# The first four output tiles of each layer computed as two pairs in Strassen's block form

## The chip, the cores and the metric

The kernel runs on one core of one Trainium2 chip. The metric is the device time of one execution in microseconds, before the change the median of three runs. A trace of one profiled execution exists beside these runs, and all durations of single instructions below come from it.

## What is computed

The reference is one inference step of a two-layer decoder trunk on 592 tokens (16 meta tokens, 512 prompt tokens, 8 x 8 sample tokens), width 1024, all in float32. Of each layer only the last two lines matter for the change:

```python
merged = jax.nn.sigmoid(g_a) * (o_a @ w_a) + jax.nn.sigmoid(g_b) * (o_b @ w_b)
return x + merged @ w_o, S_new, conv_new, h_last
```

Here `merged` is 592 x 1024, `w_o` is 1024 x 1024 and `x` the layer's input. The next layer (and the end) begins with an RMSNorm of the result, which needs the sum of squares over all 1024 features. In the second layer the 16 meta tokens are dropped, so its late stages work on 576 tokens.

## The kernel before

**Layout and precision.** Features lie on the 128 partitions: a tensor of width 1024 is 8 tiles (k = 0 to 7) of 128 features by 592 tokens. The tokens are cut in two halves of 296 (288 in the second layer), one PSUM bank per tile and half. Each float32 operand is split into a high part (rounded to the matmul's format by ScalarE) and a low part (the rest, by VectorE), and every product is three matmuls into one bank: high x high, low x high, high x low. Names: `w_raw` is the weight as loaded, `w_hi` and `w_lo` its parts; `xn_hi` and `xn_lo` hold the right operand.

**Weights.** They come in units of 1024 columns (eight 128 x 128 blocks, 512 KB) through a ring of four slots. SyncE (SP) loads unit u into its slot when unit u - 4 is done, ScalarE makes `w_hi` (L524, `split_hi`), VectorE makes `w_lo` (L531, `split_lo`), three units ahead of TensorE.

**The stages at the end of a layer**, in TensorE's order:

1. Gate stage, four pairs of tiles (`product`, L2275 to L2286). It is already in the block form: the 2 x 2 blocks of a pair's weights (A11, A12, A21, A22) and of the right operand are combined so that 7 block products of 12 matmuls take the place of 8. Sums of weight blocks are made in place: S1 and S3 by an accumulating DMA that GpSimd issues onto a block in `w_raw` (L773), S2 and S4 by VectorE (`part_add`, L1778). The combined right operands are `diff`, `mix2`, `edge` and `last_right`. The weight blocks are half units (128 x 512, 256 KB) in a ring of eight: block n is loaded when block n - 8 is done (L608), its high part is L1103 (`part_high`), its low part L1769 (`part_low`). A bank in which a partial sum stands is read before the next product is added to it.
2. Stage B: 8 tiles (m), 72 matmuls each (12 blocks x 2 halves x 3). VectorE multiplies each half by the gate out of PSUM (L1864), adds it to `acc` (L1868, this is `merged`), ScalarE makes `xn_hi` of it (L1179) and VectorE `xn_lo` (L1854, `low_merged`), one tile late.
3. Stage O, the output projection `merged @ w_o`: 8 tiles, 8 blocks x 2 halves x 3 = 48 matmuls each. Tiles 0 and 1 run interleaved (`project_first`). VectorE adds each half from PSUM, times 0.5, to x (`new_x`, L1882), which GpSimd has loaded again into `acc` (L778). Then, for the next layer, ScalarE makes `xg_hi` (L820) and the squares (L810), VectorE the low part `xg_lo` (L1240) and the running sum of squares (L1235). In the second layer the last four tiles run half by half.
4. The next layer begins with `project_first` on `xg`, and in its midst `square_sums` (L2005), which needs the sum of squares of tile 7.

Every engine works through its own list in the order written. Nothing reorders it, so an instruction that waits holds up everything behind it on its engine.

## Time and profile before

| | |
|---|---|
| median of 3 runs | 1902.77 us (1902.31 to 1903.42) |
| the profiled execution | 1901.83 us, span 1900.0 us |
| TensorE busy | 1880.8 us, 99% |
| VectorE busy | 1262.8 us, 66% |
| ScalarE busy | 807.3 us, 42% |
| GpSimd busy | 284.6 us, 15% |
| DMA, mean over the span | 136 GB/s |

The table is read from the top: TensorE is busy nearly all the time, and the others have room on average. But a matmul's row shows its whole latency of about 0.30 us, while the next one starts about 0.136 us after it, so that rows overlap. What a matmul costs is the distance between starts. An average over the span also hides that VectorE is close to full in some stages.

### The profile page before, as it was taken

Reading aid. Unit: us, or ns where it says so; the run is one execution under the profiler, and the core shown is the slowest. Engines: PE = TensorE matmul, PEld = TensorE weight load, DVE = VectorE, ACT = ScalarE, POOL = GpSimd, SP = SyncE. Lnnn points to the kernel's source line nnn. Section 1 sums busy time; section 2 is a strip of 40 time slices with the busy share of each in tenths; the row PEclk is TensorE's granted clock in tenths of the full one; section 3 lists DMA queues with packets and bytes.
Section 4 is the critical chain, followed back from the end, with each engine's and each line's share of the span. In section 5 each row is a group of like instructions: output and inputs, shape, how many; then the busy total and the mean of one; then the engine's idle time right before and its main releaser. Section 6 shows DMA issues by size and latency. Waiting matters only on the chain.

```text
span 1900.0 us, 32236 instructions
## 1 busy us (share of the span) xinstructions
PE 1880.8 (99%) x12984; PEld 1762.9 (93%) x12984; DVE 1262.8 (66%) x2144; ACT 807.3 (42%) x1293; POOL 284.6 (15%) x399
## 2 busy tenths in 40 slices
PE   8999999999999999999999999999999999999998
PEld 7899898898899999999998988988989999999997
DVE  8775665665766877864487656657557678878445
ACT  5432332423427776542344324234124377766223
POOL 2221120120231200100022201202102422001000
PEclk9999999999999999999999999999999999999999
DMA  6435544453443333543354445534544533327332
GB/s 219 129 125 166 160 149 128 164 178 110 149 150 93 107 104 97 154 124 120 99 174 158 147 124 172 178 110 149 169 126 137 165 102 111 95 83 193 103 123 78
DMA packets 114786, 257.48 MB, mean 136 GB/s; under 512 B 11822, under 2 KB 52254, under 8 KB 114510
## 3 DMA queue, kind: packets, MB, share of 16 engines
q1 hardware_dynamic: 84350, 156.00, 26.4%
q0 software_dynamic: 30144, 99.41, 16.5%
q8 instruction: 103, 1.69, 0.4%
q14 instruction: 45, 0.37, 0.1%
q10 hardware_dynamic: 144, 0.00, 0.0%
HBM read 196.55 MB, written 49.12 MB: 129 GB/s over the span
## 4 chain that ended last, share of the span: by engine, by line
PE 87%; DVE 5%; ACT 3%; DMA 2%; DVEq 1%; issue 1%; ACTq 1%; SPq 0%
PE bank L1944 20%; PE bank L1946 20%; PE bank L1945 20%; PE bank L2014 4%; PE bank L2015 4%; PE bank L2016 4%; PE last L2032 2%; DMA w_raw<-in_w_units 1%; PE last L2014 1%; PE last L2015 1%; PE last L2016 1%; PE bank L2282 1%; PE bank L2285 1%; PE bank L2284 1%; PE sums L2147 1%
## 5 line engine op out<-in xcount | busy, mean ns | idle before, releaser
L1944 PE MATMUL bank<-xn_hi,w_hi 128*128 128x296 f32 (+1 forms) x2176 | 650.8, 299 | 0.4 <-DVE w_lo L531 0.3
L1946 PE MATMUL bank<-xn_lo,w_hi 128*128 128x296 f32 (+1 forms) x2176 | 646.4, 297 | 0.0
L1945 PE MATMUL bank<-xn_hi,w_lo 128*128 128x296 f32 (+1 forms) x2176 | 645.7, 297 | 0.0
L1944 PEld LDWEIGHTS bank<-xn_hi,w_hi 128*128 128x128 f32 x2176 | 409.2, 188 | 7.0 <-issue 4.3
L1945 PEld LDWEIGHTS bank<-xn_hi,w_lo 128*128 128x128 f32 x2176 | 409.6, 188 | 1.0
L1946 PEld LDWEIGHTS bank<-xn_lo,w_hi 128*128 128x128 f32 x2176 | 408.8, 188 | 0.0
L524 ACT ACTIVATE w_hi<-w_raw 128x1024 fp32r<-128x1024 f32 x229 | 241.0, 1056 | 347.0 <-DMA w_raw<-in_w_units 344.5
L531 DVE TENSOR_TENSOR w_lo<-w_raw,w_hi 128x1024 fp32r<-128x1024 f32 x229 | 280.7, 1229 | 88.9 <-ACT w_hi L524 82.1
L1944 PE MATMUL bank<-oa_hi,w_hi 128*128 128x296 f32 (+1 forms) x512 | 153.7, 300 | 0.0
L1945 PE MATMUL bank<-oa_hi,w_lo 128*128 128x296 f32 (+1 forms) x512 | 151.9, 297 | 0.0
L1946 PE MATMUL bank<-oa_lo,w_hi 128*128 128x296 f32 (+1 forms) x512 | 151.7, 296 | 0.0
L1944 PE MATMUL bank<-ob_hi,w_hi 128*128 128x296 f32 (+1 forms) x384 | 114.0, 297 | 0.0
L1945 PE MATMUL bank<-ob_hi,w_lo 128*128 128x296 f32 (+1 forms) x384 | 113.9, 297 | 0.0
L1946 PE MATMUL bank<-ob_lo,w_hi 128*128 128x296 f32 (+1 forms) x384 | 113.8, 296 | 0.0
L2014 PE MATMUL bank<-w_hi,xn_hi 128*128 128x512 f32 x256 | 100.9, 394 | 0.7 <-DVE rot_k L1368 0.7
L2016 PE MATMUL bank<-w_lo,xn_hi 128*128 128x512 f32 x256 | 100.8, 394 | 0.0
L2015 PE MATMUL bank<-w_hi,xn_lo 128*128 128x512 f32 x256 | 100.7, 393 | 0.0
L1944 PEld LDWEIGHTS bank<-oa_hi,w_hi 128*128 128x128 f32 x512 | 96.3, 188 | 3.9 <-issue 3.9
L1945 PEld LDWEIGHTS bank<-oa_hi,w_lo 128*128 128x128 f32 x512 | 96.3, 188 | 0.0
L1946 PEld LDWEIGHTS bank<-oa_lo,w_hi 128*128 128x128 f32 x512 | 96.3, 188 | 0.0
L682 POOL DMA_DIRECT2D out_ret_s<-S x64 | 46.0, 721 | 326.1 <-DVEq L1319 180.8
L867 ACT ACTIVATE zz<-bank 128x296 f32<-128x296 f32 (+1 forms) x64 | 26.6, 416 | 132.4 <-PE bank L1946 132.4
(331 smaller groups left out, 3543.6 us busy)
## 6 DMA issues: line engine op xcount, KB each, us to landing
w_raw<-in_w_units SPq DMA_DIRECT2D x199, 512.0 KB, 3.6
S<-in_state_ret POOLq DMA_DIRECT2D x64, 512.0 KB, 4.8
out_ret_s<-S POOLq DMA_DIRECT2D x64, 512.0 KB, 6.2
w_raw<-in_w_units SPq DMA_DIRECT2D x122, 256.0 KB, 3.2
vst<-v_scr SPq DMA_DIRECT2D x8, 512.0 KB, 4.1
out_ret_p<-Sp POOLq DMA_DIRECT2D x8, 512.0 KB, 5.7
w_raw<-in_w_units POOLq DMA_DIRECT2D x16, 256.0 KB, 4.7
v_scr<-vtok_hi SPq DMA_DIRECT2D x16, 160.0 KB
```

What stands on the lines that cost most here:

```text
L524: act.activation(w_hi[:, slot(u), :], w_raw[:, slot(u), :], ACT.Copy).then_inc(unit_hi, 1)
L531: dve.tensor_tensor(w_lo[:, slot(u), :], w_raw[:, slot(u), :], w_hi[:, slot(u), :].bitcast(f32), SUB).then_inc(unit_lo, 1)
L682: pool.dma_start(dst, S[:, s, :, :]).then_inc(s_out[s], 16)
L867: act.activation(zz[:, i - 8, a:b], psum_of("R", name)[:, 0:b - a], ACT.Tanh, scale=0.5)\
L1944: pe.matmul(ps, w_hi[:, slot, cols], x_hi, start=first, stop=False)
L1945: pe.matmul(ps, w_lo[:, slot, cols], x_hi, start=False, stop=False)
L1946: return pe.matmul(ps, w_hi[:, slot, cols], x_lo, start=False, stop=last)
L2014: pe.matmul(ps, left_hi, right_hi, start=first, stop=False)
L2015: pe.matmul(ps, left_lo, right_hi, start=False, stop=False)
L2016: return pe.matmul(ps, left_hi, right_lo, start=False, stop=last)
L2032: ins = pe.matmul(o_last[at:at + QUAD, :], qz[:, c, b * QUAD:b * QUAD + QUAD], S[:, s, c, :], start=(n < 4 and c == 0), stop=(n >= 4 and c ...
L2147: pe.matmul(sums[c][:, :], ktok_hi[:, j, cols], vtok_hi[:, j, :], start=j == 0, stop=False, skip_group_check=True)
```

## The change

Stage O of both layers is cut in two. Its tiles 0 to 3 are computed as two pairs in the same block form as the gate stage (7 products of 12 matmuls for each pair of tiles). Tiles 4 to 7 stay as they were. What goes with it:

- `OUT_PAIRS = 2` pairs are added to the four of the gate stage. Their weight blocks are loaded in the order `OUT_ORDER`, with S3's block ahead of A12's, behind the last unit of stage B and ahead of the four units of tiles 4 to 7. The places in the ring now come from a table (`ring_places`), and SP waits for what held the place before.
- The right operands `diff`, `mix2`, `edge` and `last_right` are made of the merged tiles as they appear in stage B: one subtraction a tile for m = 0 to 3, three for m = 4 to 7, each with a high part on ScalarE and a low part on VectorE. The low parts of tile m - 1 are made within tile m. The last ones (of m = 7) are made beside the first products.
- VectorE adds partial sums from the banks straight into `acc` (`taken`), 14 times a layer, each behind a wait and followed by a drain. TensorE waits for them (`x_taken`) before it adds to that bank again. The order of these 14 is the table `TAKEN`.
- x is loaded again tile by tile in pairs (k, k + 4), and these transfers stand in GpSimd's list between the accumulating ones.
- For a finished tile the work for the next layer (`tile_low`, `tile_high`) and the splits of the units of tiles 4 to 7 come after the products' work.

```diff
-                                      ("O", 2, 4, four)):
+                                      ("O", 1, 4, four)):
...
+OUT_ORDER = (A11, S1, S2, S3, A12, S4, A22)
+TAKEN = ((0, A11), (0, S2), (0, S1), (0, S3), (0, S4), (1, A11), (0, A12), (0, A22),
+         (1, S2), (1, S1), (1, S3), (1, A12), (1, S4), (1, A22))
...
+            def wait_room(place):
+
+                kind, count = HELD[place - PART_RING]
+                sp.wait_ge(unit_done if kind == "unit" else part_done, count)
...
+                load_again(0)
+                add_part(TILE_PAIRS, S1)
+                load_again(1)
+                add_part(TILE_PAIRS, S3)
+                load_again(2)
+                for two in range(TILE_PAIRS + 1, LAYER_PAIRS):
+                    add_part(two, S1)
+                    add_part(two, S3)
+                load_again(3)
...
+                part_high(two, S4)
+                part_high(two, A22)
+                part_high(two + 1, A11)
+                part_high(two + 1, S1)
+                part_high(two + 1, S2)
+                part_high(two + 1, A12)
+                two += 1
+                part_high(two, S3)
+                part_high(two, S4)
+                part_high(two, A22)
+                tile_high(0)
+                split_hi(act, "O", l, 0, 0 - AHEAD)
...
+                def taken(two, product, ps, tile, part, scale, first_of=None, last_of=False):
+
+                    a, b = cut(l)[part]
+                    if first_of is not None:
+                        dve.wait_ge(x_again[tile % 4], l * 32 + 32)
+                    dve.wait_ge(part_done, l * PART_UNITS + two * PRODUCTS + product + 1)
+                    dve.scalar_tensor_tensor(acc[:, tile, a:b], ps[:, 0:wide], scale, acc[:, tile, a:b], MUL, ADD)\
+                       .then_inc(x_taken, 1)
+                    dve.drain()
...
+                taken(two, A11, x, 0, 0, 0.5, True)
+                last_of_merged(3)
+                of_merged_low(4 + 3 * 3 + 1, 3)
+                low_merged(KT - 1)
+                part_low(two, S3)
+                taken(two, S2, x, 0, 1, 0.5)
...
+                taken(two, S4, bank[2], 0, 1, 0.5)
+                part_add(two + 1, S2, S1)
+                part_low(two + 1, S1)
+                part_add(two + 1, S4, S2)
+                part_low(two + 1, S2)
+                taken(two + 1, A11, more, 2, 0, 0.5, True)
...
+                taken(two, S3, x, 3, 1, -0.5)
+                part_low(two, A22)
+                taken(two, A12, bank[3], 2, 0, 0.5)
+                taken(two, S4, bank[2], 2, 1, 0.5, None, True)
+                tile_low(0)
+                split_lo(dve, "O", l, 0, 0 - AHEAD)
+                taken(two, A22, x, 3, 0, -0.5, None, True)
+                split_lo(dve, "O", l, 0, 1 - AHEAD)
+                tile_low(1)
+                split_lo(dve, "O", l, 0, 2 - AHEAD)
...
+                for t in range(OUT_PAIRS):
+                    two, x, y, z = TILE_PAIRS + t, bank[t], bank[2], bank[3]
...
+                    wait_bank(pe, "O", l, 0, (("proj", 0), t))
+                    product(two, A11, x, xn_hi[:, 0:4, a0:b0], xn_lo[:, 0:4, a0:b0], True,
+                            mgl_ready, l * KT + 1, 1)
...
+                    product(two, S1, y, diff_hi[:, :, 0:wide], diff_lo[:, :, 0:wide], True, right_lo, at + 1, 1)
+                    wait_taken(t, A11)
+                    product(two, S2, x, mix2_hi[:, :, 0:wide], mix2_lo[:, :, 0:wide], False, right_lo, at + 5, 3)
...
+                    product(two, A12, z, xn_hi[:, 4:KT, a0:b0], xn_lo[:, 4:KT, a0:b0], True, mgl_ready, l * KT + 5, 1)
+                    wait_taken(t, S2)
+                    product(two, S3, x, edge_hi[:, :, 0:wide], edge_lo[:, :, 0:wide], False, right_lo, at + 6, 3)
+                    wait_taken(t, S1)
+                    product(two, S4, y, xn_hi[:, 4:KT, a1:b1], xn_lo[:, 4:KT, a1:b1], False)
+                    wait_taken(t, S3)
+                    product(two, A22, x, last_hi[:, :, 0:wide], last_lo[:, :, 0:wide], False, right_lo, at + 7, 3)
```

In the changed kernel the lines have other numbers: L2047 is the instruction of `taken`, L2110 that of `new_x`, L1878 `part_low`, L1887 `part_add`, L1872 the low part of a right operand, L1977 `low_merged`, L567 `split_lo`, L1349 `xg_lo` and L1344 the sum of squares.

VectorE at the start of stage O in the first layer, before: the last merged tile, then one split and the first two output tiles.

```order
L1864 SCALAR_TENSOR_TENSOR sg<-sg,bank 128x296
L1868 TENSOR_TENSOR acc<-acc,sg 128x592
L1854 TENSOR_TENSOR xn_lo<-acc,xn_hi 128x592 x2
L531 TENSOR_TENSOR w_lo<-w_raw,w_hi 128x1024
L1882 SCALAR_TENSOR_TENSOR acc<-bank,acc 128x296 x2
L531 TENSOR_TENSOR w_lo<-w_raw,w_hi 128x1024
L1240 SCALAR_TENSOR_TENSOR xg_lo<-acc,lp,xg_hi 128x592
```

VectorE now, from the second pair's `part_add` for S2 to the splits of the first two units of tiles 4 to 7.

```order
L1887 TENSOR_TENSOR w_raw<-w_raw 128x512
L1878 TENSOR_TENSOR w_lo<-w_raw,w_hi 128x512
L1887 TENSOR_TENSOR w_raw<-w_raw 128x512
L1878 TENSOR_TENSOR w_lo<-w_raw,w_hi 128x512
L2047 SCALAR_TENSOR_TENSOR acc<-bank,acc 128x296
L1878 TENSOR_TENSOR w_lo<-w_raw,w_hi 128x512
L2047 SCALAR_TENSOR_TENSOR acc<-bank,acc 128x296 x3
L1878 TENSOR_TENSOR w_lo<-w_raw,w_hi 128x512
L2047 SCALAR_TENSOR_TENSOR acc<-bank,acc 128x296
L1878 TENSOR_TENSOR w_lo<-w_raw,w_hi 128x512
L2047 SCALAR_TENSOR_TENSOR acc<-bank,acc 128x296
L1878 TENSOR_TENSOR w_lo<-w_raw,w_hi 128x512
L2047 SCALAR_TENSOR_TENSOR acc<-bank,acc 128x296 x2
L1349 SCALAR_TENSOR_TENSOR xg_lo<-acc,lp,xg_hi 128x592
L567 TENSOR_TENSOR w_lo<-w_raw,w_hi 128x1024
```

The split of the first unit (last row) was three units ahead of TensorE. It now stands behind the last products' bank reads and behind the `xg_lo` of tile 0.

GpSimd at the end of the first layer, before: the eight accumulating transfers of the gate stage, four reloads of x, the store of the new x.

```order
L773 DMA w_raw<-in_w_units 128x512 x8
L778 DMA acc<-in_x 128x1184 x4
L785 DMA x_scr<-acc 128x4736
```

GpSimd at the same place now.

```order
L813 DMA w_raw<-in_w_units 128x512 x8
L822 DMA acc<-in_x 128x592 x2
L813 DMA w_raw<-in_w_units 128x512
L822 DMA acc<-in_x 128x592 x2
L813 DMA w_raw<-in_w_units 128x512
L822 DMA acc<-in_x 128x592 x2
L813 DMA w_raw<-in_w_units 128x512 x2
L822 DMA acc<-in_x 128x592 x2
L841 DMA x_scr<-acc 128x4736
```

The four new accumulating transfers stand between the reloads, so that each waits for the reload ahead of it to be issued.

## Rows read from the trace of the kernel before

**Rows 1.** The page: busy time, TensorE's granted clock, the chain that ended last.
```profile
PE 1880.8 (99%) x12984; PEld 1762.9 (93%) x12984; DVE 1262.8 (66%) x2144; ACT 807.3 (42%) x1293; POOL 284.6 (15%) x399
...
PEclk9999999999999999999999999999999999999999
...
PE 87%; DVE 5%; ACT 3%; DMA 2%; DVEq 1%; issue 1%; ACTq 1%; SPq 0%
```

**Rows 2.** Busy time by window; us, busy us (instructions), clock, DMA share, GB/s.
```profile
781.00:827.42 46.42, 46.16 (x337) 45.60 (x336) 39.94 (x63) 33.79 (x67) 5.09 (x6) 1.00 0.73 193
827.42:905.73 78.31, 78.31 (x579) 78.31 (x578) 32.78 (x44) 18.21 (x22) 1.63 (x3) 1.00 0.32 105
905.73:958.02 52.29, 52.29 (x386) 52.29 (x385) 26.20 (x38) 17.96 (x23) 0.53 (x1) 1.00 0.29 93
1761.13:1837.61 76.48, 76.48 (x579) 76.48 (x577) 32.44 (x44) 18.11 (x22) 1.63 (x3) 1.00 0.33 107
```

**Rows 3.** Line L2282 (matmuls of products): TensorE's idle time before it, us, times.
```profile
  issue: 1.5, 4
  DVE w_lo L1769: 1.0, 3
  ACT snap L1114: 0.6, 1
```

**Rows 4.** Timeline of TensorE, end of stage B: start, duration in us, instruction.
```profile
905.59 0.30 PE L1946 MATMUL bank<-ob_lo,w_hi 128*128 128x296 f32 x1
905.73 0.30 PE L1944 MATMUL bank<-xn_hi,w_hi 128*128 128x296 f32 x1
```

**Rows 5.** Timeline of VectorE, same place.
```profile
905.92 0.46 DVE L1864 SCALAR_TENSOR_TENSOR sg<-sg,bank 128x296 f32<-128x296 f32 x1 [1.67 <-PE bank L1946]
906.48 0.78 DVE L1868 TENSOR_TENSOR acc<-acc,sg 128x592 f32<-128x592 f32 x1
...
908.97 1.23 DVE L531 TENSOR_TENSOR w_lo<-w_raw,w_hi 128x1024 fp32r<-128x1024 f32 x1 [0.17 <-ACT w_hi L524]
```

**Rows 6.** Timeline of VectorE in the gate stage.
```profile
795.33 1.59 DVE L1745 SCALAR_TENSOR_TENSOR acc<-sg,acc 128x296 f32<-128x296 f32 x4
...
804.07 0.69 DVE L1778 TENSOR_TENSOR w_raw<-w_raw 128x512 f32<-128x512 f32 x1 [1.00 <-DMA w_raw<-in_w_units]
804.85 0.69 DVE L1769 TENSOR_TENSOR w_lo<-w_raw,w_hi 128x512 fp32r<-128x512 f32 x1
```

**Rows 7.** Timeline of four engines: the third gate pair's block S1, load to matmul.
```profile
794.35 0.33 SPq L608 DMA_DIRECT2D w_raw<-in_w_units  x1
...
798.49 0.85 POOL L773 DMA_DIRECT2D w_raw<-in_w_units  x1 [5.62 <-DMA w_raw<-in_w_units]
...
804.00 0.64 ACT L1103 ACTIVATE w_hi<-w_raw 128x512 fp32r<-128x512 f32 x1 [1.49 <-DMA w_raw<-in_w_units]
...
805.69 0.38 PE L2282 MATMUL bank<-right,w_hi 128*128 128x296 f32 x1
```

**Rows 8.** Time to landing, line L608 (plain load), then L773 (accumulating).
```profile
DMA to landing us min/median/max: 2.4/3.3/5.0
...
DMA to landing us min/median/max: 3.7/4.7/5.5
```

**Rows 9.** Timeline of VectorE in stage O of the first layer and behind it.
```profile
919.80 0.83 DVE L1240 SCALAR_TENSOR_TENSOR xg_lo<-acc,lp,xg_hi 128x592 fp32r<-128x592 f32 x1
...
959.08 0.83 DVE L1882 SCALAR_TENSOR_TENSOR acc<-bank,acc 128x296 f32<-128x296 f32 x2
962.36 1.22 DVE L531 TENSOR_TENSOR w_lo<-w_raw,w_hi 128x1024 fp32r<-128x1024 f32 x1 [2.44 <-ACT w_hi L524]
963.50 0.77 DVE L1235 TENSOR_TENSOR sqs<-sqs,sq 128x592 f32<-128x592 f32 x1
```

**Rows 10.** Timeline of TensorE where the second layer begins: the last matmul ahead of the square sums.
```profile
963.45 0.29 PE L1946 MATMUL bank<-xg_lo,w_hi 128*128 128x288 f32 x1
964.32 1.26 PE L2005 MATMUL sums<-sqs,ones 128*128 128x296 f32 x4 [0.58 <-DVE sqs L1235]
```

More of the change, by code:

```diff
@@ L252, in trunk, with stored_pair @@
+def stored_pair(l, two):
+    return l * STORED_LAYER + (B_AT + 2 * two if two < TILE_PAIRS else O_AT + KT + 2 * (two - TILE_PAIRS))
+assert all(at % 2 == 0 for at in UNIT_PLACE)
 def trunk(nc, x_in, w_units, gate_w, packs, final_gain, consts, decay, state_ret,
@@ L506, in part_arrived @@
         def part_arrived(l, n):
-            return 16 * sum(1 for m in range(l + 1) for k in range(PART_UNITS if m < l else n + 1)
-                            if part_slot(m, k) == part_slot(l, n))
+            place = PART_PLACE[l * PART_UNITS + n]
+            return 16 * sum(1 for other in PART_PLACE if other <= place and (place - other) % PART_RING == 0)
         def part_of(tile, l, n):
@@ new lines, in tile_low @@
+                def tile_low(k):
+                    dve.drain()
+                    if l + 1 < DEPTH:
+                        if k == KT - 1:
+                            add_square(l + 1, k)
+                        if k == 0:
+                            dve.wait_ge(lp_in, (l + 2) * 16)
+                        gain_lo(l + 1, k)
+                        if k < KT - 1:
+                            add_square(l + 1, k)
+                    else:
+                        add_square(l + 1, k, slice(first, T))
@@ L2274, in _, with product @@
                         gates(it, g, 2)
-                def product(two, part, ps, x_hi, x_lo, start):
+                def product(two, part, ps, x_hi, x_lo, start, ready=None, count=0, step=0):
                     n = two * PRODUCTS + part
```

348 lines of the change are left out of this document (239 added, 109 removed).

## The prediction

> **What bounds the kernel now.** I read the page first: TensorE is busy for 99% of the span, at full clock, and the chain that ended last is TensorE for 87% [rows 1]. So a matmul less is time won, if nothing else becomes late. What a matmul costs I took from the windows, not from its row: stage B of the first layer is 8 x 72 = 576 matmuls in 78.31 us, 0.136 us each, and in the second layer, 288 columns wide, 576 in 76.48 us, 0.133 us [rows 2]. The 0.30 us in a row is latency, since two neighbours start 0.14 us apart [rows 4]. Then I looked for what the block form costs where the kernel already has it. In the gate stage VectorE is busy for 39.94 of 46.42 us, against 32.78 of 78.31 in stage B and 26.20 of 52.29 in stage O [rows 2]. So the change takes matmuls away and moves VectorE from half full to nearly full there. The gate stage lost 1.5 + 1.0 + 0.6 = 3.1 us ahead of its products, over eight pairs, mostly to waits for a low part [rows 3].
>
> **Removed: matmuls.** A pair of tiles took 2 x 48 = 96 matmuls and takes 7 x 12 = 84. That is 12 less for each of two pairs, 24 a layer: 24 x 0.136 = 3.26 us in the first layer, 24 x 0.133 = 3.19 us in the second, **6.45 us together**. This is all that the change can win on TensorE. A product lasts 12 x 0.136 = 1.63 us.
>
> **Added in stage B: right operands and low parts.** Per tile VectorE gets one subtraction and one low part (m below 4) or three of each (m = 4 to 7). A 296-wide operation on SBUF costs 1.59 / 4 = 0.40 us [rows 6], so at most 6 x 0.40 = 2.4 us, and with drains about 3 us, beside 32.78 / 8 = 4.1 us of 9.8 us a tile [rows 2]. Banks and units have a tile of slack. Cost: 0. Without that cover it would be the excess over 9.8 us; at 7 us there is none.
>
> **Added in stage O: hand-overs.** Bank x collects A11, S2, S3, A22 in turn, and between two of them VectorE must read it. Twice a pair the low part of the next product's weights stands right behind that read. From rows: VectorE starts 0.19 us after TensorE has started the next product (905.73 to 905.92) [rows 4, 5]; the read lasts 0.46 us, and behind a drain the next instruction starts 0.10 us after its end (906.48 against 906.38) [rows 5]; the low part lasts 0.69 us [rows 6]; TensorE starts 0.15 us after its end (804.85 + 0.69 = 805.54, and 805.69) [rows 6, 7]. Sum 1.59 us, against 1.63 us of the product that lies between. It fits with 0.04 us to spare, in the second layer (0.45 us reads, 1.59 us products) with about nothing. I take 0.1 us a layer for these.
>
> Where a rule says otherwise: a drain costs about 0.18 us by the rows. Two undrained reads take 0.83 us, so the second starts 0.37 us after the first [rows 9], where behind a drain it is 0.56 [rows 5]. The Trainium skill, VectorE: DVE Perf Modes, section The DRAIN you can't avoid, says that the next operation waits for the empty pipeline in any case, so that synchronization adds nothing. By that the three drained reads ahead of the late unit below would cost no more than plain ones, and the unit would come 0.5 us earlier. The trace differs, as said.
>
> **Added: the weight sums by accumulating DMA.** For the gate stage I followed one S1 block: its load is issued at 794.35, GpSimd issues the accumulating transfer at 798.49, it has landed at 804.00, `part_add` and the low part end at 805.54, and the matmul starts at 805.69, 0.04 us later than the spacing of matmuls asks, plus about 0.07 us for the next start [rows 6, 7]. That is 11.3 us of chain, and the ring gives the same seven products, 7 x 1.63 = 11.4, less 0.19. In the change only S1 of the second pair has this schedule. S3's block is now loaded one product earlier (ahead of A12), so it has 1.6 us of cover, and the gate stage's largest waits were at S3. Block sums of the first pair are loaded tiles ahead, in stage B. Bounds for the one tight chain: landings of 2.4 to 5.0 and 3.7 to 5.5 us [rows 8] make it 0 to 2.5 us late; at the medians 0.1. I take 0.15 us a layer. With the hand-overs that is **0.5 us** for both layers; by the gate stage's rate, 3.1 / 8 a pair, four pairs would pay 1.55 us.
>
> **Moved: the split of the first plain unit.** Before, it was made three units ahead. Now VectorE reaches it late. Count from t, the start of the last S4 product: TensorE wants the unit two products later, at t + 3.26. VectorE: the read of S3 starts at t + 0.19 and takes 0.46 + 0.10; A22's low part 0.61 (0.69, the next one overlapping by 0.08); the read of A12 0.56; the read of S4 0.56, whose product has ended at t + 1.82, when VectorE is at t + 1.92; `xg_lo` of tile 0, 0.75 (0.83 [rows 9] less the overlap); the split 1.23 [rows 5]; TensorE starts 0.15 later. Sum: 0.19 + 0.56 + 0.61 + 0.56 + 0.56 + 0.75 + 1.23 + 0.15 = 4.61. Doubled drains and the extra semaphore instruction add some 0.1. So TensorE waits 4.7 - 3.26 = **1.45 us** in the first layer. ScalarE has the high part in time: the unit's room is free when the second A11 is done, some ten us before. In the second layer there is no `xg_lo` (tile 0's square needs no addition), and products are 0.04 shorter: 3.9 - 3.2 = **0.7 us**. The other units follow with room, since a unit feeds 48 matmuls (6.5 us) in the first layer and 24 (3.2 us) in the second, against a split of 1.23 and a few short operations.
>
> **Given back at the end of the first layer.** There TensorE waits today: the square sums start 0.87 us after the matmul ahead of them, instead of 0.14 [rows 10]. The reason is a late VectorE: stage O ends at 958.02, the read of its last tile could start 0.2 us later but the pair starts at 959.08, and from there it is read, square, gain, split, addition to 964.27 [rows 9]. In the change tiles 4 to 7 keep the spacing of 6.5 us a tile, and VectorE with ScalarE need 963.50 - 959.08 = 4.42, plus 0.69 for the addition and 0.75 for the gain, 5.9 us a tile [rows 9]. The backlog (tiles 2 to 5) is worked off by tile 6. Then the last half is read at once and its sum is ready 4.81 us after that read begins (964.27 - 959.46), 5.0 us after the end of stage O, while TensorE asks for it after 5.57 (963.59 - 958.02). The wait of 0.73 us goes: **-0.75 us**. What is late next there is the same addition, with 0.5 us of room. In the second layer there is no such place.
>
> **The sum.** -6.45 + 0.5 + 1.45 + 0.7 - 0.75 = -4.55 us. Against the profiled execution of 1901.83 us that is 1897.3; the median of the runs shown lies 0.94 higher, at 1902.77, and gives **1898.2 us**, -0.24%. Loads and SP: seven half units replace four halves' worth of two tiles, plus two accumulating ones, at a DMA share of 0.29 in stage O against 0.73 in the gate stage [rows 2]; the reloads of x are now eight smaller ones, the last behind the second pair's S3 transfer, and are needed some 3 us after landing. SP waits longer for room ahead of the four plain units, but behind it stand only units for the next layer, needed 25 us later. Cost 0.
>
> **Rivals.**
> - *Hand-overs cost what they cost in the gate stage, or more.* Every product in the two pairs waits for a read, a low part or both, with 0.0 to 0.5 us of room, so small delays add up: if six of the fourteen hand-overs a layer miss by 0.2 us, that is 2.4 us more, 1900.6 us, within 0.2% of before. For it: VectorE's list from the end of stage B to the split (14 reads of 0.56, 10 low parts of 0.61, 2 block sums of 0.79, four drained operations for tile 7, the last right operands, `xg_lo`, the split) sums to about 21.8 us of 24. Against it: in the gate stage nothing but the S1 and S3 chains shows.
> - *The late unit is not late, or its wait is half.* If VectorE's reads overlap as undrained ones do, three times 0.18 us and the doubled drains go, and the terms 1.45 and 0.7 shrink to some 0.85 and 0.1: 1897.0 us.
> - *The accumulating transfer becomes the bound.* `part_add` of the second pair waits in VectorE's list for S1's transfer, and behind it stand the reads of A11, A12 and A22, so the whole pair moves. It is slower than before from 2.3 us more per layer on, that is a load and a transfer together 2.6 us over the medians; the largest landings seen add 2.5 us. For slower by 0.2% each layer must lose 4.2 us more: 1907 us. Its place in GpSimd's list behind a reload that waits for the merged tiles could do that, but those merged tiles are there 10 us before.
> - *The clock falls.* A full stretch of the pairs at the lower of the two levels (1.2 instead of 2.4 GHz) would double it, +22.8 us a layer, 1943 us in all; 9 us at the lower level cancel the gain. The granted clock is 1.00 through the gate stage, with the same kind of gaps, and right behind the 0.87 us gap of rows 10 [rows 1, 2, 10]. The Trainium skill, TensorE: Matmul & The Clock Gate, section on psum-queue depth-cycling, warns of just this form: short idle times between bursts as banks are cycled, and a clock that swings. The trace speaks against it.
>
> **How the numbers follow.** A run of this kernel can tell about 0.2%, 3.8 us, from no change: the line is at 1899.0. Forecast (1897.6 to 1898.95) 0.44; the half-late unit 0.16; hand-overs and chains 0.33, of which about 0.03 lie below the line; accumulating DMA slower than before 0.05; clock 0.02. Faster: 0.44 + 0.16 + 0.03 = 0.63, slower by 0.2% 0.03, within 0.2% 0.34. The range that leaves 0.1 out at each end: from 1896.4, where every stall but the late unit's half is gone, to 1901.3 (forecast plus 3.1), where the tight chain is 2 us late in one layer and hand-overs cost the gate stage's rate.
>
> **What would show it.** After: 12936 matmuls; TensorE idle before the first plain unit of tiles 4 to 7, put down to the low part of L567, about 1.4 us in the first layer and 0.7 in the second; next to nothing in front of products but at S1 of the second pair; no wait at the square sums; stage O 52.29 - 3.26 + 1.7 = 50.7 us long in the first layer. The prediction is wrong if idle time shows at several products of a pair (hand-overs), if S1 or S3 of the second pair waits over 1 us (DMA), or if the square sums still wait (then VectorE's backlog lasts to the end).

## The result and the profile after

Before and after were run in turn on one chip, 13 times each: 1902.65 us before (1901.59 to 1903.47), **1906.08 us after** (1901.83 to 1907.99). The ratio is 1.0016, 95% interval [1.0009, 1.0024]. The change makes the kernel 0.16% slower. It was predicted to make it 0.24% faster; the sign is wrong and the time lies outside the range. Single executions of the change spread over 6.2 us, those of before over 1.9, so an explanation from one trace is tested below by changing the kernel. The profiled execution took 1905.52 us, with a span of 1903.6 us, 3.6 more than before.

The page first, the line that answers to the first of [rows 1].

```profile
PE 1876.4 (99%) x12936; PEld 1757.6 (92%) x12936; DVE 1310.2 (69%) x2250; ACT 825.2 (43%) x1345; POOL 295.8 (16%) x415
```

There are 48 matmuls less, as reckoned, and TensorE's busy time fell by 4.4 us while the span grew. So time is lost between matmuls or in slower ones. The waits of TensorE say where (line, what it waited for, us in total, times, longest).

```profile
PE bank L2507 <- DVE acc L2047: 4.9, 2, 2.5
PE bank L2167 <- DVE w_lo L567: 1.7, 2, 1.2
...
PE bank L2507 <- DVE w_lo L1878: 1.3, 2, 1.1
PE sums L2228 <- DVE sqs L1344: 1.2, 2, 1.0
```

The first row is new, stands once in each layer, and is larger than everything that the prediction had in stage O. (Most of the 1.3 us of L1878 lies in the gate stage of the second layer.) On TensorE's timeline of the first layer it is the start of product S2 of the second pair; then the first plain unit and the square sums.

```profile
919.97 0.30 PE L2510 MATMUL bank<-right,w_hi 128*128 128x296 f32 x1
922.65 0.61 PE L2507 MATMUL bank<-right,w_hi 128*128 128x296 f32 x1 [2.39 <-DVE acc L2047]
923.06 0.45 PE L2509 MATMUL bank<-right,w_lo 128*128 128x296 f32 x1
923.31 0.45 PE L2510 MATMUL bank<-right,w_hi 128*128 128x296 f32 x1
...
925.77 0.31 PE L2507 MATMUL bank<-xn_hi,w_hi 128*128 128x296 f32 x1
925.92 0.30 PE L2509 MATMUL bank<-xn_hi,w_lo 128*128 128x296 f32 x1
...
932.18 0.30 PE L2510 MATMUL bank<-last_lo,w_hi 128*128 128x296 f32 x1
933.73 0.41 PE L2167 MATMUL bank<-xn_hi,w_hi 128*128 128x296 f32 x1 [1.25 <-DVE w_lo L567]
...
965.35 0.29 PE L2169 MATMUL bank<-xg_lo,w_hi 128*128 128x288 f32 x1
965.82 0.52 PE L2228 MATMUL sums<-sqs,ones 128*128 128x296 f32 x1 [0.18 <-DVE sqs L1344]
```

The distance from start to start is what counts. It is 2.68 us ahead of S2. Behind it come one step of 0.41 us and then steps of 0.24 to 0.25 us (923.06 to 923.31, and so on), twelve matmuls in all, and at 925.77 the spacing is back at 0.14. The windows name the reason (us; busy us of the engines; granted clock, DMA share, GB/s): stage O of the first layer, the pause, and the stretches behind it in both layers.

```profile
905.41:959.92 54.51, 50.88 (x363) 50.39 (x362) 37.09 (x60) 22.41 (x33) 2.88 (x4) 0.97 0.44 128
...
919.97:922.65 2.68, 0.29 (x3) 0.05 (x1) 1.76 (x3) 1.69 (x3) 0.00 (x0) 0.94 0.97 384
922.65:925.77 3.12, 3.12 (x12) 3.12 (x13) 1.54 (x3) 2.56 (x4) 0.00 (x0) 0.50 0.05 21
...
1856.35:1861.04 4.69, 4.69 (x23) 4.69 (x24) 3.71 (x7) 4.14 (x6) 0.00 (x0) 0.64 0.35 94
```

**Behind the pause the granted clock is 0.50: TensorE runs at the lower of its two levels, 1.2 GHz.** The 12 matmuls take 3.12 us instead of 12 x 0.136 = 1.63, 1.49 us more. In the second layer the pause is 2.81 us (1853.54 to 1856.35), and the 23 matmuls behind it take 4.69 instead of 23 x 0.133 = 3.06, 1.63 us more.

Now the account closes. First layer: stage O lasted 52.29 us [rows 2] and lasts 54.51, +2.22. The terms are -3.26 (24 matmuls), +2.54 (2.68 less one spacing), +1.49 (lower clock), +1.41 (933.73 - 932.18 less one spacing): +2.18. Second layer: -3.19 + 2.68 + 1.63 + 0.62 = +1.74. The square sums wait 0.40 us less. Together +3.5, against +3.6 in the spans. What is left over is small and cancels: stage O starts 0.32 us earlier than before, and about 0.4 us more is spent elsewhere, 0.2 of it in the second gate stage.

### The profile page after: what moved, and what is told of

Its sections match the earlier page's. It is cut to its first block, busy times and chain, and to the rows that moved or that the text cites. A ratio compares the mean times of both kernels' runs of the same rounds, so it can differ in the third digit from the quotient of the medians.

```text
span 1903.6 us, 32423 instructions
## 1 busy us (share of the span) xinstructions
PE 1876.4 (99%) x12936; PEld 1757.6 (92%) x12936; DVE 1310.2 (69%) x2250; ACT 825.2 (43%) x1345; POOL 295.8 (16%) x415
## 4 chain that ended last, share of the span: by engine, by line
PE 86%; DVE 5%; ACT 3%; DMA 2%; DVEq 1%; issue 1%; ACTq 1%; SPq 0%
PE bank L2167 19%; PE bank L2169 19%; PE bank L2168 19%; PE bank L2237 4%; PE bank L2238 4%; PE bank L2239 4%; PE bank L2507 2%; PE bank L2510 2%; PE bank L2509 2%; PE last L2255 2%; DMA w_raw<-in_w_units 1%; PE last L2237 1%; PE last L2238 1%; PE last L2239 1%; PE sums L2370 1%
## 5 line engine op out<-in xcount | busy, mean ns | idle before, releaser
L2167 PE MATMUL bank<-xn_hi,w_hi 128*128 128x296 f32 (+1 forms) x2048 | 613.1, 299 | 1.9 <-DVE w_lo L567 1.7
L2169 PE MATMUL bank<-xn_lo,w_hi 128*128 128x296 f32 (+1 forms) x2048 | 608.4, 297 | 0.0
L2168 PE MATMUL bank<-xn_hi,w_lo 128*128 128x296 f32 (+1 forms) x2048 | 607.6, 297 | 0.0
L2167 PEld LDWEIGHTS bank<-xn_hi,w_hi 128*128 128x128 f32 x2048 | 385.0, 188 | 9.0 <-issue 4.3
L2168 PEld LDWEIGHTS bank<-xn_hi,w_lo 128*128 128x128 f32 x2048 | 385.5, 188 | 1.0
L2169 PEld LDWEIGHTS bank<-xn_lo,w_hi 128*128 128x128 f32 x2048 | 384.6, 188 | 0.0
L560 ACT ACTIVATE w_hi<-w_raw 128x1024 fp32r<-128x1024 f32 x221 | 232.2, 1055 | 344.5 <-DMA w_raw<-in_w_units 342.0
L567 DVE TENSOR_TENSOR w_lo<-w_raw,w_hi 128x1024 fp32r<-128x1024 f32 x221 | 270.8, 1228 | 69.2 <-ACT w_hi L560 62.4
```

What stands on the lines that cost most here:

```text
L560: act.activation(w_hi[:, slot(u), :], w_raw[:, slot(u), :], ACT.Copy).then_inc(unit_hi, 1)
L567: dve.tensor_tensor(w_lo[:, slot(u), :], w_raw[:, slot(u), :], w_hi[:, slot(u), :].bitcast(f32), SUB).then_inc(unit_lo, 1)
L2167: pe.matmul(ps, w_hi[:, slot, cols], x_hi, start=first, stop=False)
L2168: pe.matmul(ps, w_lo[:, slot, cols], x_hi, start=False, stop=False)
L2169: return pe.matmul(ps, w_hi[:, slot, cols], x_lo, start=False, stop=last)
```

## Why S2 waits

TensorE waits for VectorE's read of bank x (L2047). VectorE's timeline at that place:

```profile
917.32 0.69 DVE L1878 TENSOR_TENSOR w_lo<-w_raw,w_hi 128x512 fp32r<-128x512 f32 x1
920.74 0.69 DVE L1887 TENSOR_TENSOR w_raw<-w_raw 128x512 f32<-128x512 f32 x1 [2.73 <-DMA w_raw<-in_w_units]
921.53 0.69 DVE L1878 TENSOR_TENSOR w_lo<-w_raw,w_hi 128x512 fp32r<-128x512 f32 x1
922.14 0.46 DVE L2047 SCALAR_TENSOR_TENSOR acc<-bank,acc 128x296 f32<-128x296 f32 x1
```

The read itself isn't late, it is queued. Ahead of it stands `part_add(two + 1, S4, S2)` (L1887), which needs the loaded block of **S4**. It must stand ahead of the low part of S2 (L1878), which is written over the raw block that the addition reads. So the load of S4, whose own product comes three products later, holds up the low part of S2 and the bank that S2 adds to. Behind the landing come 0.79 + 0.61 + 0.51 us of VectorE, and TensorE wants S2 at 920.10: the block has to be there by 918.2. Its issue on SyncE, and GpSimd's issues beside it:

```profile
913.76 1.96 SPq L647 DMA_DIRECT2D w_raw<-in_w_units  x3
```

```profile
913.62 0.86 POOL L813 DMA_DIRECT2D w_raw<-in_w_units  x1 [1.09 <-DMA w_raw<-in_w_units]
914.18 1.42 POOL L822 DMA_DIRECT2D acc<-in_x  x2
```

SyncE's three are A12 (913.76), S4 (914.1) and A22 (915.4); GpSimd's are S3's accumulating transfer and the reload of tiles 3 and 7. The landing of A12's and S4's loads, the two in the window from 914.0:

```profile
DMA to landing us min/median/max: 6.1/6.3/6.6
```

S4's 6.6 us, against a median of 3.3 and a longest of 5.0 for such loads in the gate stage [rows 8]: 914.1 + 6.6 = 920.7. At 3.3 it would have been there at 917.4, 0.8 us in time. Between 913.6 and 915.4 four blocks of 256 KB and two tiles of 296 KB were asked for, 1.6 MB.

Three candidates for the length: the accumulating transfer, the reload of x, and S4's place in the ring. Both pairs load in the order A11, S1, S2, S3, A12, S4, A22, while TensorE multiplies S3 after A12. A12's load of the second pair takes the place of the first pair's S3, S4's takes the place of A12, which was done a product earlier. SyncE issues in order, so S4 stands behind the wait for S3, and both loads go out at once.

## Experiments

Times are medians with lowest and highest, the ratio is to the kernel before on the same chip in the same session.

### The reload of x made small

```diff
-                        pool.dma_start(acc[:, m, :], (x_in if l == 0 else x_scr[l - 1])[:, m * T:m * T + T])\
+                        w = T if k < 3 else 8
+                        pool.dma_start(acc[:, m, 0:w], (x_in if l == 0 else x_scr[l - 1])[:, m * T:m * T + w])\
```

> In this kernel the last reload of x (tiles 3 and 7) moves 8 of the 592 columns of each tile; the rest of those two tiles keeps the merged values, so their part of the result is left out. Theory T (transfers compete): in the changed kernel the load of the second pair's S4 block was issued at 914.1 and landed 6.6 us later, because it shared the DMA with the reload of tiles 3 and 7 (0.6 MB) and S3's accumulating transfer; part_add waits for it, and behind it in VectorE's list stand S2's low part and the read of A11, so TensorE stood still for 2.5 us ahead of S2. Without the reload the load lands in 3.5 to 4.5 us, the wait falls from 2.5 to 0.3 to 0.8 us a layer, the granted clock stays at the upper level, and the time is 1897.5 to 1899.5. Rival Q (the load is issued too late, and the reload does not matter): landing stays above 5.5 us, the wait above 2 us, 1905 to 1906. Rival V (VectorE's list is full): the wait stays above 2 us although the load has landed.

Measured: 1906.07 us (1904.5 to 1908.8), ratio 1.0019 [1.0009, 1.0028]. A12's and S4's loads landed (two loads, one window):

```profile
DMA to landing us min/median/max: 5.7/5.9/6.1
```

```profile
923.17 0.30 PE L2511 MATMUL bank<-right,w_hi 128*128 128x296 f32 x1
925.37 0.41 PE L2508 MATMUL bank<-right,w_hi 128*128 128x296 f32 x1 [1.91 <-DVE acc L2048]
```

S4 lands 0.5 us sooner, the pause is 2.20 instead of 2.68 us (1.96 instead of 2.81 in the second layer), and no stretch at the lower clock follows. The reload alone isn't the cause. That the time didn't move although so much went is taken up at the end of this section.

### The loads in another order

```diff
-OUT_ORDER = (A11, S1, S2, S3, A12, S4, A22)
+OUT_ORDER = (A11, S1, S2, S3, S4, A12, A22)
...
-    return range(PRODUCTS) if two < TILE_PAIRS else OUT_ORDER
+    return range(PRODUCTS) if two <= TILE_PAIRS else OUT_ORDER
...
-                        part_high(TILE_PAIRS, S3)
...
+                part_high(two, S3)
```

The first pair loads in the order of the products, the second has S4 ahead of A12, so S4 now takes the place of the first pair's A12, one product sooner. The high part of S3 of the first pair moves behind the merged tiles on ScalarE.

> The first pair's weight blocks are loaded in the order of the products, the second pair's as A11, S1, S2, S3, S4, A12, A22, so that the second pair's S4 block finds its room one product earlier (after the first A12, about 912.2 instead of 914.1) and ahead of the last reload. Everything is still moved. Theory T or Q alike: the load lands by 917, the wait ahead of S2 is under 0.3 us, the clock stays up, 1896.5 to 1898.5; A12's block, now the later one, lands late but before its product (0 to 0.5 us of wait). Rival V: VectorE is still late, the wait ahead of S2 is above 1 us, above 1903.

Measured: **1899.67 us** (1898.4 to 1908.2), ratio 0.9989 [0.9979, 0.9999], 6.4 us less than the change. S4's load, issued at 912.9:

```profile
DMA to landing us min/median/max: 3.3/3.3/3.3
```

The wait at S2 and the lower clock are gone in both layers, with everything still moved. The time is 1.2 us above the expected range. A smaller pause stands one product earlier, at S1 (0.85 us in the first layer, 0.53 in the second); in the first layer its load now took 4.9 us and its accumulating transfer 5.1, against 4.1 each in the change:

```profile
919.10 0.30 PE L2510 MATMUL bank<-xn_lo,w_hi 128*128 128x296 f32 x1
919.95 0.38 PE L2507 MATMUL bank<-right,w_hi 128*128 128x296 f32 x1 [0.56 <-issue]
```

### The reload of tile 7 later

```diff
+                        if m == KT - 1:
+                            pool.wait_ge(x_again[3], l * 32 + 16)
+                            pool.wait_ge(part_in[part_slot(l, (LAYER_PAIRS - 1) * PRODUCTS + A22)],
+                                         part_arrived(l, (LAYER_PAIRS - 1) * PRODUCTS + A22))
...
-                        dve.wait_ge(x_again[tile % 4], l * 32 + 32)
+                        dve.wait_ge(x_again[tile % 4], l * 32 + (32 if tile != 3 else 16))
...
+                    if i == 3 and n == 0:
+                        dve.wait_ge(x_again[3], l * 32 + 32)
```

> Only the reload of tile 7 is moved: it is issued after tile 3's has landed and the second pair's last block is in. Loads keep their order and their times of issue. Theory T: half of the competing bytes go, S4's load lands in 4.5 to 5.3 us instead of 6.6, the wait falls from 2.5 to 0.8 to 1.4 us a layer, and with it most of the time at the lower clock: 1898.5 to 1901. Rival Q: the wait stays above 2 us, 1905 to 1906.5.

Measured: 1906.03 us (1903.58 to 1909.43), ratio 1.0018 [1.0008, 1.0027]. With half the reload out of the way S4 took 7.0 us, and the pause was 3.13 us in the first layer (920.48 to 923.61). Nothing was won, as rival Q had it.

```profile
923.61 0.40 PE L2513 MATMUL bank<-right,w_hi 128*128 128x296 f32 x1 [2.83 <-DVE acc L2051]
```

One thing in this trace goes against the account of the clock. In the second layer the pause was 2.98 us (1855.53 to 1858.51), longer than in the change, and the 24 matmuls behind it took 3.26 us at full clock:

```profile
1858.51:1861.77 3.26, 3.26 (x24) 3.25 (x25) 2.79 (x6) 2.25 (x4) 0.56 (x1) 1.00 0.53 123
```

So a pause of this length can bring the clock down and need not.

### Load order, later reload and the split first

The edits of the last two, and on VectorE the split of the first plain unit ahead of `xg_lo`:

```diff
-                tile_low(0)
                 split_lo(dve, "O", l, 0, 0 - AHEAD)
+                tile_low(0)
```

> The edits of e2 and e3 together, and the split of the first plain unit ahead of tile 0's xg_lo. Theory T: no wait ahead of the second pair's S2, no time at the lower clock, the wait ahead of the first plain unit 0.5 us in the first layer instead of 1.3, 1895.5 to 1897.5. Rival V: above 1900, with waits at several products.

Measured: 1900.44 us (1897.43 to 1902.38), ratio 0.9986 [0.9977, 0.9995]. The pause at the first plain unit fell from 1.55 to 0.67 us. Against the load order alone nothing is to be told apart in the times.

### The accumulating transfer made small

```diff
+                    w = 8 if (two, part) == (LAYER_PAIRS - 1, S3) else 4 * P
-                    pool.dma_start(part_of(w_raw, l, n), w_units[stored_pair(l, two) + m]
-                                   [:, k * 4 * P:k * 4 * P + 4 * P], accum_op=ADD)\
+                    pool.dma_start(part_of(w_raw, l, n)[:, 0:w], w_units[stored_pair(l, two) + m]
+                                   [:, k * 4 * P:k * 4 * P + w], accum_op=ADD)\
```

> The changed kernel, but the accumulating transfer of S3's block of the second output pair moves 8 of its 512 columns (so that product lacks most of its second addend; its issue, wait and semaphore stay). Theory A (the accumulating transfer, in flight with A12's and S4's loads, is what stretches S4's landing from 3.3 to 6.6 us): S4 lands in about 4 us, the TensorE wait ahead of S2 (2.4 and 2.5 us) falls under 0.3 us, the stretch at the lower clock goes with it, time about 1906.1 - 6.0 = 1900 us. Theory B (the load stands too late behind the release of its slot, and A12's load, issued 0.3 us ahead of it, plus the reload of x do most of the stretching): S4 still lands in 5.5 us or more, the wait stays at 1.3 us or more, time about 1904.5 us or more.

Measured: 1901.62 us (1899.85 to 1903.16), ratio 0.9993 [0.9984, 1.0002]. A12 and S4 in the first layer:

```profile
DMA to landing us min/median/max: 4.6/5.2/5.8
```

```profile
923.36 0.40 PE L2508 MATMUL bank<-right,w_hi 128*128 128x296 f32 x1 [1.64 <-DVE acc L2048]
```

A pause of 1.93 us in the first layer, none in the second, and the clock stays up. It lies between the two theories: the time is 4.5 us less than the change's and S4 lands 0.8 us sooner, more than with the reload small, yet S4 still takes 5.8 us.

### S4 ahead of A12, and nothing else

```diff
-OUT_ORDER = (A11, S1, S2, S3, A12, S4, A22)
+OUT_ORDER = (A11, S1, S2, S3, S4, A12, A22)
```

> The changed kernel with one word moved: both output pairs load their blocks as A11, S1, S2, S3, S4, A12, A22, so that S4's block goes out 0.35 us ahead of A12's instead of behind it. If place in the queue of loads decides (theory B), S4 lands 1 us or more earlier than the 920.7 us of the changed kernel, the wait falls to about 1.2 us a layer and the time to about 1903.5 us, with A12 now late but needed 1.6 us later. If the transfers only share the same engines (theory A), both loads still land within 0.3 us of each other at about 920.4 us, the wait is 2.1 us or more and the time 1905.3 us or more.

Measured: 1904.51 us (1902.66 to 1905.16), ratio 1.0006 [0.9996, 1.0015]. S4's load, issued at 913.6, 0.5 us earlier and with A12's 1.6 us behind it:

```profile
DMA to landing us min/median/max: 5.5/5.5/5.5
```

S4 landed at 919.1, 1.6 us sooner than in the change, as theory B had it. S2 starts 1.26 us after the matmul ahead of it instead of 2.68, and now A12 is late (7.2 us to landing): 1.53 us ahead of its product in the first layer, 2.24 in the second, and there the clock falls again.

```profile
1856.41 0.46 PE L2507 MATMUL bank<-xn_hi,w_hi 128*128 128x288 f32 x1 [1.95 <-DVE acc L2047]
...
1859.80 0.40 PE L2510 MATMUL bank<-right,w_hi 128*128 128x288 f32 x1
```

Swapping two neighbours in the crowd moves the wait from one block to the other. The 1904.5 us against 1899.7 of the order above is what the place in the ring does: there S4's load takes the place of the first pair's A12 and goes out at 912.9, one product ahead of A12's (914.5) and two ahead of A22's (916.2).

### A pause put in

On the kernel with the new load order (no wait at S2, full clock), in the first layer only:

```diff
                     wait_taken(t, A11)
+                    if t == 1 and l == 0:
+                        pe.wait_ge(xgh_ready, KT + 1)
                     product(two, S2, x, mix2_hi[:, :, 0:wide], mix2_lo[:, :, 0:wide], False, right_lo, at + 5, 3)
```

> The kernel with the new load order (1899.7 us, no wait ahead of the second pair's S2, no stretch at the lower clock), and in layer 1 one more TensorE wait there: S2 of the second pair starts only when the high part of xg of tile 0 is made, 2.6 us later. Theory C (a TensorE pause of this length brings the granted clock down to its lower level for the next dozen matmuls and costs 1.3 us on top of itself): the starts behind the pause are 0.24 to 0.25 us apart for about 12 matmuls and the time is 1899.7 + 2.6 + 1.3 = 1903.6 us. Rival (the slow matmuls of the changed kernel come from the heavy DMA traffic of 300 to 350 GB/s at that time, not from the pause): starts stay 0.136 us apart behind the pause and the time is 1902.3 us.

Measured: 1904.85 us (1902.89 to 1906.54), ratio 1.0008 [0.9999, 1.0017], 5.2 us above the kernel without it. Timeline and window:

```profile
922.15 0.30 PE L2510 MATMUL bank<-right,w_hi 128*128 128x296 f32 x1
925.49 0.58 PE L2507 MATMUL bank<-right,w_hi 128*128 128x296 f32 x1 [3.04 <-issue]
925.87 0.45 PE L2509 MATMUL bank<-right,w_lo 128*128 128x296 f32 x1
```

```profile
925.49:928.59 3.10, 3.10 (x13) 3.10 (x14) 0.00 (x0) 2.70 (x4) 0.00 (x0) 0.50 0.00 0
```

The pause is 3.34 us from start to start, and the 12 matmuls from there to 928.59 take 3.10 us instead of 1.63. The DMA share is 0.00 in that window, so traffic beside them isn't needed to slow them, and the kernel without the put-in wait, with the same transfers, stays at full clock. Of the 5.2 us the trace shows 3.2 of pause and 1.5 of clock. The rival falls: it is the pause, though the 2.98 us above show that such a pause doesn't always do it.

### The split first, with the new load order

The edit of VectorE's list above, without the later reload.

> The kernel with the new load order (1899.7 us), and of the VectorE list one swap: the split of the first plain unit stands ahead of the low part of xg of tile 0. The pause ahead of the first plain unit was 1.52 - 0.14 = 1.38 us in layer 1 there; xg's low part takes 0.6 us, so 0.7 to 0.9 us of it go and the time is 1899.7 - 0.8 = 1898.9 us. The later reload of tile 7, the other half of the kernel that had both, is expected to be worth nothing or a loss of under 0.5 us. Rival: what was gained is given back at the sum of squares, since xg's low parts come later: 1899.7 us.

Measured: 1899.94 us (1896.89 to 1905.26), ratio 0.9984 [0.9975, 0.9993]. Whether the 0.8 us are there the times can't tell: by the medians nothing, by the ratios 1 us, both within the intervals. In the trace the unit's pause did shrink, from 1.53 to 0.68 us in the first layer, but S1 of the second pair, 0.85 us in the kernel that this one is built on, paused for 1.72 in this execution (which took 1901.75 us, 1.8 above the median), its load having taken 6.0 us:

```profile
919.03 0.30 PE L2510 MATMUL bank<-xn_lo,w_hi 128*128 128x296 f32 x1
920.75 0.38 PE L2507 MATMUL bank<-right,w_hi 128*128 128x296 f32 x1 [1.42 <-issue]
```

The granted clock stayed at 1.00 behind it.

### S1 first

```diff
-OUT_ORDER = (A11, S1, S2, S3, S4, A12, A22)
+OUT_ORDER = (S1, A11, S2, S3, S4, A12, A22)
```

on the kernel before this one (the first pair again in the order of the products).

> The kernel with the new load order and the split ahead of xg's low part (1899.9 us; in its profiled execution TensorE starts S1 of the second pair 1.72 us after the matmul ahead of it, in both layers, since S1's load was issued 907.9 and landed 6.0 us later). One more swap: the second pair loads S1's block ahead of A11's. S1's load then goes out one place earlier, at about 906.7, its sum has landed by about 917 instead of 919.1, and both pauses go: -1.5 us each, so about 1897.4 us, a gain over before of about 5 us, which the interval shows as below 1. Rival: S1's load lands just as late beside the two loads it now shares the engines with, or A11, now issued later, becomes the late one: 1899.5 to 1900 us.

Measured: **1898.07 us** (1896.04 to 1899.79), ratio 0.9978 [0.9968, 0.9987]. It beats both kernels, 4.5 us less than before and about 8 less than the change. Of the two pauses at S1 the first layer's is gone; in the second 0.84 us of 1.71 stay. In the first layer one pause over 0.27 us is left in stage O, the first plain unit's, and the stage is as short as the removed matmuls allow but for that:

```profile
905.48:955.03 49.55, 49.17 (x362) 48.93 (x361) 37.04 (x60) 22.84 (x34) 2.88 (x4) 1.00 0.52 152
```

```profile
928.86 0.40 PE L2167 MATMUL bank<-xn_hi,w_hi 128*128 128x296 f32 x1 [0.38 <-DVE w_lo L567]
```

52.29 - 3.26 + 0.54 = 49.57, measured 49.55. So VectorE's drained hand-overs between products cost nothing that can be seen there.

### Both transfers small

The small accumulating transfer and the small reload together, on the change.

> The changed kernel with two transfers of its crowded stretch made small at once: the accumulating one of S3 of the second output pair (8 of 512 columns) and the last reload of x (8 of 592 columns of tiles 3 and 7). One at a time they left S4's landing at 5.8 us (accumulating one small) and 6.1 us (reload small), against 6.6 with both whole and 3.3 reckoned. If the transfers add up (256 KB and 592 KB beside 768 KB of loads), S4 lands within 4.5 us, the wait ahead of S2 is under 0.3 us in both layers, the lower clock doesn't show, and the time is about 1900 us. If even then S4 lands after 5.5 us, the loads of A12, S4 and A22 slow each other, the wait stays over 1 us and the time is about 1902 us.

Measured: 1899.54 us (1897.59 to 1900.18), ratio 0.9984 [0.9974, 0.9993]. A12 and S4:

```profile
DMA to landing us min/median/max: 4.0/4.2/4.4
```

The pause ahead of S2 is 0.44 us in the first layer (0.30 over a spacing) and 0.60 in the second, and the clock stays up. Both transfers matter: S4 takes 6.6 us with both whole, 6.1 without the reload, 5.8 without the accumulation, 4.4 without either. The two savings alone (0.5 and 0.8) don't make 2.2, so either one that is left keeps most of the delay.

### The sum of squares ahead of the split

```diff
+                    if i < 3:
+                        split_lo(dve, "O", l, 0, i)
-                    split_lo(dve, "O", l, 0, i)
                     for k in ((), (4, 5), (6,), (7,))[i]:
                         tile_low(k)
+                    if i == 3:
+                        split_lo(dve, "O", l, 0, i)
```

on the kernel with S1 first.

> The kernel with S1 first (see there), and at the end of the first layer the last addition to the sum of squares and xg's low part stand ahead of the split of the last plain unit in VectorE's list. In the changed kernel that addition starts at 964.99 although its square was made at 962.0, since the split of 1.23 us stands ahead of it. Expected: no TensorE idle time put down to the sum of squares where the second layer begins (0.33 us above the spacing before), the unit's split, 1.5 us later, still ahead of its use, so 0.3 us less than the kernel with S1 first; too small for the times to show, the trace must. Rival: the pause at the square sums stays at 0.47 us, as it did in every variant, because it belongs to the change of the matmul's operand.

Measured: 1898.45 us (1896.77 to 1901.32), ratio 0.9982 [0.9973, 0.999]. TensorE at the square sums:

```profile
961.73 0.29 PE L2172 MATMUL bank<-xg_lo,w_hi 128*128 128x288 f32 x1
961.86 1.16 PE L2231 MATMUL sums<-sqs,ones 128*128 128x296 f32 x4
```

The pause is gone (0.13 us instead of 0.47), so the rival falls; in the times 0.3 us doesn't show, as expected.

### The small reload again

The first experiment with 16 columns instead of 8. Its expectation gives the gate stages' pauses as 6.9 and 3.4 us; added up again they are 6.1 in the first experiment and 2.7 in the change.

> The kernel with the last reload small once more (16 columns of tiles 3 and 7 instead of 8). The first time its trace showed 1.0 us less TensorE wait ahead of the two S2 products and no stretch at the lower clock (3.1 us in the changed kernel), so about 4 us less there, and yet the same time as the changed kernel, 1906.07 us: its gate stages, whose work the edit doesn't touch, had lost 6.9 us in pauses of over 0.3 us, against 3.4 us in the changed kernel. If the gate stage's loss varies from one execution to the next with the landing of its accumulating transfers, this run's gate stages lose 3 to 4 us again and its time comes out near 1903 us. If it belongs to the build (6 us or more again), its time is 1906 us again.

Measured: 1903.86 us (1902.41 to 1907.46), ratio 1.0007 [0.9998, 1.0016]. S4's landing is 6.2 us, the pause ahead of S2 2.33 us in the first layer (with 13 matmuls at the lower clock behind it) and 0.52 in the second. Its gate stages lost 4.3 us. So two kernels that differ by 8 columns differ by 2.2 us in their medians and by 1.8 us in the gate stages' pauses of one execution each. What makes these vary is open: it was seen in one profiled execution of each only.

The traces can be compared without the gate stages. Stage O of the first layer plus the stretch from the start of the second layer's stage O to the end took 118.8 us in the change and 114.7 before. The small reload has 114.6 and, the second time, 114.8; the small accumulating transfer 112.4, both small 111.4; the new load order 112.0, S1 first 110.5. So the reload is worth about 4 us there, twice, and in the first experiment the gate stages and what lies between took it back.

## Why the prediction was wrong

- **The sum's last paragraph ("Loads and SP ... Cost 0") failed.** It took DMA as free from a mean share over the whole of stage O in the kernel before (0.29), which says nothing of 1.6 MB asked for within 2 us. It looked at when the reloads were needed, not at what they do to the loads beside them. In place of 0 the runs show 2.54 + 2.68 us of pause, and the lower clock behind it. With the same bytes moved and S4's load a product earlier the pause is gone, so the term hangs on when a load goes out beside what, not on the share of DMA that is busy.
- **"In the change only S1 of the second pair has this schedule" failed.** The chain was followed for S1 and S3, the accumulated blocks, and not for S4, a plain load, which has no accumulating transfer behind it but goes out as late as the first pair's S3 allows, and whose block sum stands ahead of the low part and the bank read of S2 in VectorE's list. The rows for it were at hand: the longest plain landing in the gate stage was 5.0 us [rows 8], and S4 had 4.1 us. The tight chain that was foreseen, S1's, showed no pause in the changed kernel.
- **The clock.** This rival had a chance of 0.02, because gaps of up to 0.87 us had left the clock alone [rows 2, 3, 10]. The wait for S4 made a longer one, and the clock behind it cost 1.49 + 1.63 us. The put-in pause shows that such a pause is enough; why 2.98 us once left the clock up stays open. The Trainium skill, TensorE: Matmul & The Clock Gate, in its section on psum-queue depth-cycling, describes idle times between groups of matmuls, and a re-throttle paid between bursts. Here the traces agree in part: the many short hand-overs of the banks didn't do it (with S1 first, the stage's 49.55 us have a clock of 1.00), single long pauses did.
- **Which rival came.** None as written. The accumulating transfer's was nearest: right that a block sum in VectorE's list holds up the bank reads behind it, and in its size (it had slower than before from 2.3 us a layer), wrong in the block, and it had 0.05. The wait itself, 2.5 and 2.7 us, would still have ended near before's time; the clock's 3.1 us make it slower. Of the signs named for being wrong, only the square sums came; none looked for a wait at S2.
- **Matmuls (-6.45): right.** 12936 matmuls, and the account closes with that term.
- **Added work in stage B at no cost: right.** Stage B of the first layer takes 78.31 us as before (827.10 to 905.41).
- **Hand-overs (0.1 us a layer): right**, if anything too high. No product of the two pairs starts more than 0.27 us after the matmul ahead of it in the change, in either layer, but S2.
- **The late first plain unit (1.45 and 0.7): right.** Measured 1.41 and 0.62 above the spacing. The working priced each drained read at 0.56 us. By the prediction's reading of the Trainium skill, VectorE: DVE Perf Modes, section The DRAIN you can't avoid (synchronization adds nothing), the unit would have come 0.5 us earlier; it didn't. What that section measured are semaphores between operations, not an explicit drain as in this kernel, and it also says that an operation that isn't held starts earlier.
- **The square sums (-0.75): half right.** The pause went from 0.87 to 0.47 us. The step "the backlog is worked off by tile 6, then the last half is read at once" failed. VectorE's list there:

```profile
957.64 1.23 DVE L567 TENSOR_TENSOR w_lo<-w_raw,w_hi 128x1024 fp32r<-128x1024 f32 x1 [2.44 <-ACT w_hi L560]
958.97 0.83 DVE L1349 SCALAR_TENSOR_TENSOR xg_lo<-acc,lp,xg_hi 128x592 fp32r<-128x592 f32 x1
959.72 0.77 DVE L1344 TENSOR_TENSOR sqs<-sqs,sq 128x592 f32<-128x592 f32 x1
960.40 0.83 DVE L2110 SCALAR_TENSOR_TENSOR acc<-bank,acc 128x296 f32<-128x296 f32 x2
...
963.68 1.23 DVE L567 TENSOR_TENSOR w_lo<-w_raw,w_hi 128x1024 fp32r<-128x1024 f32 x1 [2.44 <-ACT w_hi L560]
964.99 0.77 DVE L1344 TENSOR_TENSOR sqs<-sqs,sq 128x592 f32<-128x592 f32 x1
```

VectorE had no backlog at all: it idles 2.44 us ahead of each split, for ScalarE's high part of the unit, and [rows 9] already had that 2.44. The split waits, and the additions stand behind it. What looked like a lack of time was an order, and moving the addition ahead of the split took the pause away.

## What to carry to other kernels

Where an engine's list mixes work on several blocks, find for each block the *first* instruction that touches it, not the product that uses it: a block sum can make a load urgent two or three products earlier. Give loads in a ring the order in which their places come free as well as that in which they are needed, and space them; swapping neighbours in a crowd moved most of the wait, while letting S4's load go out a product earlier was worth 5 to 6 us here. And price a late transfer with the longest landing in the rows plus what else is in flight then, and a pause of TensorE of two to three microseconds with the lower clock behind it, about 1.6 us more here.

## What the runs showed of the hardware

- A load of 256 KB from memory landed in 3.3 us when it went out a product ahead of the next load (the new load order), and S4's in 6.6 us in both layers of the change, within 2 us of an accumulating transfer of 256 KB, a reload of 592 KB and two other loads, which themselves took 4.6 to 7.7 us. With the transfer and the reload small, the three loads of the first layer took 3.8 to 4.4 us.
- Pauses of TensorE and the clock behind them in stage O: 1.71, 1.72, 1.93, 1.96 and 2.20 us left it at 1.00, and so did 2.98 us. Behind 2.24, 2.33, 2.68, 2.81, 3.13 and 3.34 us 12 to 15 matmuls ran at 0.50, 0.24 to 0.25 us apart, at a cost of 1.5 to 1.6 us each time. The fall can come later than the pause: behind the 2.81 us of the change's second layer the first nine matmuls still took 1.34 us together, before 14 slow ones. These are single executions.
- Builds of nearly the same kernel differed by 2.2 us in their medians, half of what this change was to bring. A difference of under 2 us between two kernels needs the trace, not the time.
